# A routed-expert kernel's TensorE loop with its two phases exchanged, the last routing tile in another order, and the final scaling regrouped

## The reference, cut to what matters

```python
# x: (1024, 1024) after the mixer; E = 32 experts, D = F = 1024
tokens = rms_norm(x, g_pre_ffn) * (1.0 + sc2) + sh2
logits = tokens @ w_router + b_router
top_val, top_idx = lax.top_k(logits, 4)
top_w = softmax(top_val)
# for each expert e, over the rows that chose it:
gate = minimum(xb @ w_gate[e] + b_gate[e], 7.0)
up = clip(xb @ w_up[e] + b_up[e], -7.0, 7.0)
h = (up + 1.0) * gate * sigmoid(1.702 * gate)
y[row] += top_w * (h @ w_down[e] + b_down[e])
...
x = x + gt2 * rms_norm(y, g_post_ffn)
```

## Time and profile before

| what | value |
|---|---|
| time, median of 3 runs | 2397.28 us (2397.16 to 2398.49) |
| the profiled execution: time | 2394.5 us |
| its span, first to last instruction | 2392.6 us |
| PE busy / PEld / DVE / ACT / POOL | 2221.9 (93%) / 1176.8 / 1043.4 / 668.5 / 376.6 us |
| mean granted TensorE clock | 0.969 |
| the chain that ended last | PE 85%, DMA 6%, DVE 4% |
| of which lines 1753 and 1786 | 40% and 19% |
| routing, then first gate phase | about 725 us, 807.22 us |
| last TensorE phase begins, last VectorE instruction begins | 2330.48 us, 2386.10 us |

### The profile page before, as it was taken

The page is one execution under the profiler, slowest core; times in us unless marked ns, Lnnn a source line. Parts: engine busy times, 40 slices in busy tenths (PEclk is TensorE's granted clock), DMA queues, the critical chain, the costliest instruction groups (busy, mean ns, idle before and its releaser), DMA issues.

```text
span 2392.6 us, 57077 instructions
## 1 busy us (share of the span) xinstructions
PE 2221.9 (93%) x21767; PEld 1176.8 (49%) x21768; DVE 1043.4 (44%) x1664; ACT 668.5 (28%) x1414; POOL 376.6 (16%) x491
## 2 busy tenths in 40 slices
PE   5999999998996599999999999999998999999982
PEld 3485765867454244545445454444443444444441
DVE  4154547445346344434434443443353444433334
ACT  5111222233344332222322222322232222222222
POOL 5000000000014212111111121111122112211111
PEclk9999999999997699999999999999999999999996
DMA  9112011126205294967979788888887897888864
GB/s 302 35 36 72 26 33 48 31 67 246 93 36 202 90 373 127 360 211 279 338 250 344 251 313 314 287 305 287 286 328 272 303 340 271 309 291 337 322 216 157
DMA packets 187702, 525.54 MB, mean 220 GB/s; under 512 B 20330, under 2 KB 68066, under 8 KB 187490
## 3 DMA queue, kind: packets, MB, share of 16 engines
q1 hardware_dynamic: 133874, 338.86, 37.7%
q10 hardware_dynamic: 36240, 134.29, 14.4%
q0 software_dynamic: 17536, 51.69, 9.6%
HBM read 486.21 MB, written 38.57 MB: 219 GB/s over the span
## 4 chain that ended last, share of the span: by engine, by line
PE 85%; DMA 6%; DVE 4%; issue 1%; ACT 1%; POOL 1%; ACTq 0%; SPq 0%; POOLq 0%; DVEq 0%
PE ps L1753 40%; PE ps L1786 19%; PE ps L1536 6%; PE ps L1637 5%; PE ps L1532 5%; DMA w_gu_e<-in_w_up_dram 4%; PE ps L1542 2%; PE ps L1593 2%; PE ps L1539 2%; PE ps L1615 1%; PE ps L1656 1%; PE ps L1508 1%; DMA w_down_e<-in_w_down_dram 1%; DVE box L1107 0%; DVE y_all L1460 0%
## 5 line engine op out<-in xcount | busy, mean ns | idle before, releaser
L1753 PE MATMUL ps<-w_gu_e,xT 128*32 128x512 f32 x9216 | 1007.7, 595 | 34.3 <-DVEq L1418 16.6
L1753 PEld LDWEIGHTS ps<-w_gu_e,xT 128*32 128x32 f32 x9216 | 355.9, 110 | 667.4 <-issue 667.1
L1786 PE MATMUL ps<-w_down_e,hT 128*32 128x256 f32 x9216 | 508.7, 380 | 13.4 <-ACT yrow L932 8.4
L1786 PEld LDWEIGHTS ps<-w_down_e,hT 128*32 128x32 f32 x9216 | 351.3, 110 | 181.8 <-issue 40.8
L1383 DVE STREAM_TRANSPOSE gu_t<-ps 128x1024 f32<-128x1024 f32 x94 | 111.9, 1229 | 639.4 <-PE ps L1753 639.4
L914 ACT ACTIVATE xT<-xr,fm 128x128 f32<-128x128 f32 x392 | 184.1, 490 | 569.0 <-PE ps L1753 544.6
L1369 DVE TENSOR_SCALAR yrow<-ps,slot_tab 32x256 f32<-32x256 f32 x376 | 181.3, 482 | 259.0 <-PE ps L1786 167.9
L932 ACT ACTIVATE yrow<-ps,slot_tab 32x256 f32<-32x256 f32 x384 | 179.4, 467 | 352.2 <-issue 235.9
L655 POOL DMA_INDIRECT xg<-xn_rows,idx_g x196 | 197.4, 1007 | 85.4 <-issue 47.6
L649 POOL TENSOR_TENSOR idx_g<-slot_tab,base_row 128x4 int32<-128x4 int32 x49 | 9.2, 189 | 1101.6 <-DVE xr L1405 1087.5
L1536 PE MATMUL ps<-hxT,w_ring 128*128 128x512 f32 (+1 forms) x384 | 142.5, 529 | 3.7 <-ACT hxT L802 3.7
(11 more groups left out here) (301 smaller groups left out, 1515.2 us busy)
## 6 DMA issues: line engine op xcount, KB each, us to landing
w_gu_e<-in_w_gate_dram SPq DMA_DIRECT2D x256, 512.0 KB, 10.7
w_gu_e<-in_w_up_dram SPq DMA_DIRECT2D x256, 512.0 KB, 11.6
w_down_e<-in_w_down_dram ACTq DMA_DIRECT2D x124, 1024.0 KB, 9.2
w_ring<-in_w_ada_dram SPq DMA_DIRECT2D x17, 1024.0 KB, 5.2
w_ring<-in_w_in_dram SPq DMA_DIRECT2D x20, 512.0 KB, 5.2
w_first<-in_w_ada_dram SPq DMA_DIRECT2D x7, 1024.0 KB, 12.2
x_all<-in_x_dram SPq DMA_DIRECT2D x2, 2048.0 KB, 10.6
w_out<-in_w_out_dram SPq DMA_DIRECT2D x8, 512.0 KB, 8.6
```

The costliest lines, as they stand in the source:

```text
L1753: last = T.matmul(ps[j * GROUP:(j + 1) * GROUP, g, :].rearrange("p (w b f) -> p w b f", w=2, f=GROUP), xT[:, k, g * GROUP:(g + 1) * GROUP] ...
L1786: last = T.matmul(ps[j * GROUP:(j + 1) * GROUP, 4 + g // 2, g % 2 * QUARTER:(g % 2 + 1) * QUARTER], hT[:, g, k, :], w_dn[:, k, j * QUARTER ...
```

## The change

- **TensorE's loop**: a round runs `gate_up` first and `down` after it, so down belongs to the item one round back. One round fewer is run, the packed table is shifted by one place, and the waits at the head of each phase compare with a register one higher (`n + 1`, `2 * m + 2`), for which ScalarE and VectorE add the missing counts beforehand. The wait for `y0_ready` ahead of the loop becomes the first gate's wait for `gu_evac`.
- **`gate_up`** tests for size 1 first; its code stands directly behind the loop's head.
- **Routing**: TensorE turns the last tile before `places(5)` and `logits(6)`; VectorE runs `place(5)` ahead of `choose(6)`; ScalarE takes the exponentials of tile 5 before the last tile's move out of PSUM, and leaves out the square root that it ran in the last round to change tables; GpSimd puts the slots of tiles 5, 6 and 7 before it adds up their weights.
- **The end**: `y` times gain is written to a buffer of its own (`yg_all`) as tiles land, by VectorE for six tiles and by GpSimd for tiles 5 and 6; one VectorE instruction per tile then multiplies by the root and adds to `x1`.

```diff
         y_all = region(0, 32)("y_all", TL, D)
...
-        FIN_POOL = (2, 4, 6)
+        FIN_POOL = (5, 6)
+        FIN_EARLY = (2, 4, 8, 8)
...
-            return eng.value_load(int_n[0:1, 2:3], min_val=NE + 2, max_val=ITEMS + 2)
+            return eng.value_load(int_n[0:1, 2:3], min_val=NE + 1, max_val=ITEMS + 1)
...
-            for t in range(TL):
+            for t in range(TL - 3):
                 put_slots(t)
+                spread_weights(t)
+            for t in range(TL - 3, TL):
+                put_slots(t)
+            for t in range(TL - 3, TL):
                 spread_weights(t)
...
             for t in FIN_POOL:
-                pool.wait_ge(fin_scaled, t + 1)
-                G.tensor_tensor(x1[:, t, :], x1[:, t, :], y_all[:, t, :], ALU.add).then_inc(fin_pool, 1)
+                pool.wait_ge(y_in[t], 16)
+                G.tensor_tensor(yg_all[:, t, :], y_all[:, t, :], gain[1][:], ALU.mult).then_inc(fin_pool, 1)
...
                 if t >= 3:
                     exponents(t - 3)
+                if 3 <= t < TL - 1:
                     A.activation(rs_s[:, 39:40], ones[:, 0:1], ACT.Sqrt)
+            exponents(TL - 3)
             transposed_tile(TL - 1)
-            for t in range(TL - 3, TL):
+            for t in range(TL - 2, TL):
                 exponents(t)
...
             first_rows(4)
+            act.sem_inc(gu_evac, 2)
...
+            place(TL - 3)
             choose(TL - 2)
-            place(TL - 3)
             choose(TL - 1)
...
-            V.tensor_copy(int_q[:, 0:2], tab_q[:, 0:2])
-            V.scalar_tensor_tensor(out=int_q[:, 2:NTAB], in0=tab_w[:, 0:NTAB - 2], scalar=8.0, in1=tab_q[:, 2:NTAB],
+            V.tensor_copy(int_q[:, 0:1], tab_q[:, 0:1])
+            V.scalar_tensor_tensor(out=int_q[:, 1:NTAB], in0=tab_w[:, 0:NTAB - 1], scalar=8.0, in1=tab_q[:, 1:NTAB],
...
-                dve.wait_ge(gu_evac, m * 2 + 2)
+                dve.wait_ge(gu_evac, m * 2 + 4)
...
+            def gained(lo, hi):
+
+                for t in range(lo, hi):
+                    if t not in FIN_POOL:
+                        dve.wait_ge(y_in[t], 16)
+                        V.tensor_tensor(yg_all[:, t, :], y_all[:, t, :], gain[1][:], ALU.mult).then_inc(fin_gained, 1)
...
             for g, (lo, hi) in enumerate(FIN):
+                gained(FIN_EARLY[g - 1] if g else 0, FIN_EARLY[g])
...
-                    V.scalar_tensor_tensor(out=y, in0=y, scalar=rstd[:, t:t + 1], in1=gain[1][:], op0=ALU.mult,
-                                           op1=ALU.mult).then_inc(fin_scaled, 1)
-                    if t not in FIN_POOL:
-                        dve.wait_ge(fin_scaled, t + 1)
-                        V.tensor_tensor(x1[:, t, :], x1[:, t, :], y, ALU.add).then_inc(fin_dve, 1)
...
+                    V.scalar_tensor_tensor(out=x1[:, t, :], in0=yg_all[:, t, :], scalar=rstd[:, t:t + 1],
+                                           in1=x1[:, t, :], op0=ALU.mult, op1=ALU.add).then_inc(fin_dve, 1)
...
-                if 1 <= t < TL:
+                if 1 <= t <= TL:
                     turned_rows(t - 1)
+                if t == TL:
+                    places(t - 3)
                 if 2 <= t < TL + 2:
                     logits(t - 2)
-                if t >= 3:
+                if t >= 3 and t != TL:
                     places(t - 3)
-                if t == TL:
-                    turned_rows(t - 1)
...
-                pe.wait_ge(gu_evac, m * 2)
+                pe.wait_ge(gu_evac, m * 2 + 2)
                 apart(pe)
...
+                with pe.If(size == 1):
+                    gate_up_of(m, loaded, (0,), True)
...
-                pe.wait_ge(hT_ready, n)
-                pe.wait_ge(yr_ready, n)
-                pe.wait_ge(yv_ready, n)
+                pe.wait_ge(hT_ready, n + 1)
+                pe.wait_ge(yr_ready, n + 1)
+                pe.wait_ge(yv_ready, n + 1)
...
-            pe.wait_ge(y0_ready, 2 * TL)
             with pe.Fori(0, n_rounds) as n:
                 pair = item_pair(pe, n)
+                gate_up(n, ((pair >> 6) & 63) * 32, pair & 7)
                 down(n, (pair >> 12) * 16, (pair >> 3) & 7)
-                gate_up(n, ((pair >> 6) & 63) * 32, pair & 7)
```

More of the change, by code:

```diff
@@ L533, in _ @@
             for t in range(TL):
-                if t in FIN_POOL:
-                    sp.wait_ge(fin_pool, FIN_POOL.index(t) + 1)
-                else:
-                    sp.wait_ge(fin_dve, sum(u not in FIN_POOL for u in range(t + 1)))
+                sp.wait_ge(fin_dve, t + 1)
                 sp.dma_start(out[0, t * P:(t + 1) * P, :], x1[:, t, :]).then_inc(out_done, 16)
@@ L1338, in _ @@
                             tab_it[:].unsqueeze(2).to_broadcast([P, 4, NTAB]), ALU.mult).then_inc(diag_tab, 1)
-            for k, more in enumerate((-1.0, -2.0, 2.0)):
+            for k, more in enumerate((-1.0, -2.0, 1.0)):
                 V.tensor_scalar(int_n[:, k:k + 1], n_items[:], more, None, ALU.add)
@@ L1458, in _ @@
                 for t in range(lo, hi):
[L1459 to L1464 removed]
+                    if t in FIN_POOL:
+                        dve.wait_ge(fin_pool, FIN_POOL.index(t) + 1)
+                    else:
+                        dve.wait_ge(fin_gained, sum(u not in FIN_POOL for u in range(t + 1)))
+                    V.scalar_tensor_tensor(out=x1[:, t, :], in0=yg_all[:, t, :], scalar=rstd[:, t:t + 1],
+                                           in1=x1[:, t, :], op0=ALU.mult, op1=ALU.add).then_inc(fin_dve, 1)
         @block.tensor
```

28 lines of the change are left out of this document (13 added, 15 removed).

## The result

The changed kernel takes 2454.63 us (median of 4, 2453.12 to 2457.07), against 2397.22 for the one before (2395.63 to 2398.49) on the same chip: a ratio of 1.0239, 95% interval 1.0224 to 1.0254. That is 57.4 us more where 38.7 were forecast, and 0.6 us above the upper end of the range. The direction and the mechanism of the loop were right; the term of the start was not.

A forecast was written before the change was run, and what follows sets the result against it. TensorE's gate and down matmuls, some 1516 of 2392.6 us, were taken to bound the kernel. Loop +49, start -7.5 and end -3 gave +38.5 us, so 2436 us (+1.6%); 2412 to 2454 held 8 in 10.

The forecast's parts named there:

- the term of the start: Routing and first rounds: earlier rows and no jump before the first gate phase, -7.5 us, between -11 and -3.
- The lead and the seam: Down to gate: 3.0 us of sequencer work less 1.1 of lead leaves 1.9; gate to down stays at 0.4.
- The lead of 32 matmuls: Rival at the down-to-gate seam: a longer lead, so each seam grows by only 0.84 us, time 2416; chance 0.05.
- The loop's sum: All 45 down-to-gate seams: 61.2 us added less 12 taken back, +49 us, between +29 and +63.
- 13 us came back: Loop: 12 us given back where phases wait anyway, 8 in gate phases waiting for weights, 4 in down phases.
- The extra test: Gate phase's entry: the test for size 1 adds one taken branch, 0.3 us, at seams where it is taken.
- the tables: Routing: turning the last tile earlier makes the tables end 2.6 us earlier, at 781.5.
- of this 12.9 us most is lent: First gate phase: starts at 794.3 for 807.22, but the jumps come after it, so most of the gain is lost.
- 794.3 + 6.5 + 8.2 + 3.6: Second gate phase's start: first start, matmul issue, two branches, other sequencer work; 812.6 against 820.29, 7.7 us earlier.
- The end: Final scaling after the last down matmul: fewer GpSimd operations and overlaps, -3 us, between -5 and 0.
- The code doesn't stay: Rival in the loop: one branch per round costs 3.6 us again, 46 rounds add 166 us, 2600; chance 0.03.

The follow-up runs named there:

- the old tests: The changed kernel with the gate phase's size tests in their old order, more than one block first: 2430.89 us, ratio 1.0134.
- both cures: The changed kernel with the size tests in their old order and the next round's pair read inside the down phase: 2399.00 us, ratio 1.0011.
- the moved loop: The changed kernel with its loop moved in memory, first instruction 128 instructions behind the start of a 16 KB piece: 2444.95 us, ratio 1.0195.
- the end-alone kernel: The kernel before with nothing but the new order of the final scale factors, run on the slower chip: ratio 0.9996.

## Why the prediction was wrong

- **The lead and the seam: right.** A gap of 1.9 us was forecast, 1.82 came; gate to down stayed at 0.38. The same arithmetic (sequencer work less a lead of some 1.1 us) then gave the gaps of three kernels ahead of their runs: 1.5 (1.56 measured), 0.8 to 0.9 (0.68) and 0.4 (0.41). The gap of 1.9 us cost no clock, as forecast (granted 1.00 over 1000 to 2300 in both kernels). The lead of 32 matmuls, the prediction's estimate from the queue of 64 that the Trainium skill gives TensorE (Advanced Engine Details and Errata, Engine Queue Depths), is out: it would have left gaps of 0.42 + 0.84 = 1.26 us.
- **The loop's sum: right, 49 forecast, 47 to 48 measured.** The gaps behind down phases grew by 60 us in all, where 61.2 were forecast, and 13 us came back, where 12 were. The extra test is 8 us of it. They came where the forecast had them: the four waits of 1.8 to 2.0 us behind short gate phases became 0.9 to 1.1, and the wait for the up weights fell from 11.1 us to 3.9.
- **The start: this step failed.** -7.5 us were forecast, between -11 and -3; +10 to +11 came. The first gate phase did start without a jump, 10.8 and 11.8 us earlier (12.9 forecast), and the tables were 2.5 us earlier (2.6 forecast). What failed is the sentence "of this 12.9 us most is lent", with its sum 794.3 + 6.5 + 8.2 + 3.6. It took two jumps from the earlier trace rows where the changed path has three (3.4 us more). The path before has three as well, but the row of the third isn't in the earlier trace rows:

```profile
L1775 PEldq COMPARE_BRANCH  x1: 3159/3159/3159, 798.1 to 798.1; - x1
```

With that the second gate phase started 1.7 and 2.9 us earlier and not 7.7. Worse, the sum ended there, as if code once reached were paid for. Five pieces were paid for twice: from the second to the third gate phase it took 12.9 and 12.6 us longer than before. The stops of 6.1 and 5.3 us that make this up were in no term, bound or rival, and half clock around them (0.57 from 858 to 870, 1.00 before) made them dearer. The three experiments with no hole on this stretch show what the term would have been: -4.4 us with the old tests, which also put one jump where rows are waited for, -6.0 with both cures, and -2.2 with the moved loop.

- **The end: right in sign**, -2 for -3. It can't be told from no change alone.
- **"The code doesn't stay" was taken too lightly.** That rival got 0.03, since the code had the same length. The length wasn't the question. Two stops of that kind did come, and 192 instructions of shift brought the rival itself, at 3025 us. The Trainium skill (Advanced Engine Details and Errata, ISA Cache) gives TensorE 128 KB in lines of 16 KB, 256 instructions each; that is eight lines, and the runs agree in so far as 7 pieces stay and 8 do not. Its "Only 2 cache lines!" is not what they show.

## What to carry to other kernels

Ask of each instruction between two phases in which seam it stands, and how many instructions the sequencer is ahead there: behind short matmuls the same lead is worth half the time, and register work moved into the middle of a phase gained about as much here (6 to 7 us) as the parts of the change that gained anything. Count the pieces of code that a long loop touches and how often each is fetched; with the same work done, another order of three tests was worth 24 us here, and another place of the loop in memory cost 570. When a jump is taken out of one round, follow the path through the next two rounds too.

## What the runs showed that I had not expected

- A piece of code jumped over before it is fetched makes everything behind it be fetched again when it is reached: 38 fetches for 33, some 11 us at the start. That the loaded code must be one unbroken stretch is my reading of it; the counts of 33, 35, 38 and 39 fit, but no run shows the store itself.
- A loop of 1643 instructions runs in 2455 us if it touches 7 pieces of 16 KB and in 3025 if it touches 8.
- One chip takes 30 us longer than the others on the same kernel (2427.9 against 2397.0 to 2399.5). There the down phases are longer (their matmuls are busy 542 us in the end-alone kernel's page, 509 in that of before), matmuls of two phases often interleave, and a seam of the same sequencer work shows a shorter gap (0.16 for 0.42). Why wasn't looked into.
- A value read by TensorE's sequencer in the middle of a phase took 0.3 us in most rounds and 1.1 in a few.
- The part ahead of the loop differs by up to 6.9 us between profiles (637.3 to 644.2 for the first tile). The two profiles with the least half clock ahead of 635 us, 20 us, have 637.3; those with 27 to 34 us have 639 to 644.
